# Three reorderings in a fused transformer kernel: shift after the first matmuls, attention steps of a mixer and of two layers

## The reference

```python
def first_block(...):                     # one layer
    mod = silu(c) @ w_ada + b_ada         # 9 vectors of 1024
    sh1, sc1, gt1, sh2, sc2, gt2, sh3, sc3, gt3 = split(mod)
    u = rmsnorm(h, g_norm_ffn1) * (1 + sc1) + sh1
    h = h + 0.5 * gt1 * swiglu(u, w_ffn1_in, w_ffn1_out)     # F = 2816
    u = rmsnorm(h, g_norm_mix) * (1 + sc2) + sh2
    h = h + gt2 * token_mixing(u, ...)    # pooling, and attention in 3 groups x 4 heads
    u = rmsnorm(h, g_norm_ffn2) * (1 + sc3) + sh3
    h = h + 0.5 * gt3 * swiglu(u, w_ffn2_in, w_ffn2_out)
    return rmsnorm(h, g_final)

def second_block(...):                    # two layers
    ret_o = retention(...)                # 4 heads, group norm: (o - mean) / sqrt(var + eps)
    swa_o = sliding window attention with sinks   # 6 query heads
    mla_o = latent attention, rope on 32 of 96 columns   # 6 heads
    x = layer_norm(ALPHA * x + concat(ret_o, swa_o, mla_o) @ w_out)
    x = layer_norm(ALPHA * x + grouped_moe(x))    # 16 experts, top 2
```

## Time and profile before

| | |
|---|---|
| median of 3 runs | 1138.8 us |
| lowest, highest | 1138.6, 1139.92 us |
| the profiled execution | 1139.93 us |
| its span in the trace | 1138.1 us |
| mean granted PE clock | 0.987 |
| PE busy | 1082.3 us |
| DVE busy | 876.1 us |
| ACT busy | 632.7 us |
| POOL busy | 90.1 us |

### The profile page before, as it was taken

How to read it: one execution, slowest core, us unless ns; L and a number is a source line. 1 busy time by engine, 2 the same in 40 slices (tenths; PEclk the granted TensorE clock), 3 DMA queues, 4 the chain that set the end, 5 groups by cost and what they waited for, 6 DMA issues and landing times.

```text
span 1138.1 us, 24969 instructions
## 1 busy us (share of the span) xinstructions
PE 1082.3 (95%) x10736; PEld 820.4 (72%) x10736; DVE 876.1 (77%) x1130; ACT 632.7 (56%) x792; POOL 90.1 (8%) x104
## 2 busy tenths in 40 slices
PE   6999999999889999999999998999989998999996
PEld 5777776688668477777678674877758876497773
DVE  4799799788667885555668856999966875699994
ACT  1554344454446564344466545878745754687872
POOL 1115611061000110000000000000000000000000
PEclk9999999999989999999999999999999999999998
DMA  9999799565436678655545225599994422569991
GB/s 340 372 368 374 268 344 360 177 218 187 161 135 223 201 254 285 219 193 161 152 166 203 77 75 226 181 384 414 414 281 128 158 100 86 222 223 398 416 374 39
DMA packets 134718, 271.94 MB, mean 239 GB/s; under 512 B 9429, under 2 KB 98105, under 8 KB 126297
## 3 DMA queue, kind: packets, MB, share of 16 engines
q1 hardware_dynamic: 124248, 231.79, 57.1%
q0 software_dynamic: 7904, 29.25, 7.3%
q10 hardware_dynamic: 2464, 9.44, 2.2%
HBM read 269.41 MB, written 1.05 MB: 238 GB/s over the span
## 4 chain that ended last, share of the span: by engine, by line
PE 77%; DVE 13%; ACT 4%; DMA 3%; issue 3%; ACTq 0%; DVEq 0%; SPq 0%
PE ps L750 64%; DVE wlo L469 4%; PE ps L1625 3%; DMA area<-in_w_ada_dram 2%; PE ps L1673 1%; PE ps L892 1%; PE ps L902 1%; DVE area L2842 1%; PE ps L910 1%; PE ps L1278 1%; DVE bnst L2283 1%; PE ps L1087 1%; PE ps L1290 1%; ACT area L1776 1%; PE ps L1125 0%
## 5 line engine op out<-in xcount | busy, mean ns | idle before, releaser
L469 DVE SCALAR_TENSOR_TENSOR wlo<-raw,whi 128x2048 f16<-128x2048 f32 (+4 forms) x212 | 466.4, 2231 | 31.6 <-ACT whi L444 31.0
L444 ACT ACTIVATE whi<-raw 128x2048 f16<-128x2048 f32 (+4 forms) x212 | 385.3, 1849 | 26.4 <-DMA raw<-in_w_ffn_in_dram 10.2
L750 PE MATMUL ps<-uhi,whi 128*128 128x256 f16 (+2 forms) x1328 | 329.8, 260 | 3.1 <-DVE ulo L2309 2.0
L750 PE MATMUL ps<-ulo,whi 128*128 128x256 f16 (+2 forms) x1328 | 329.6, 260 | 0.0
L750 PE MATMUL ps<-uhi,wlo 128*128 128x256 f16 (+2 forms) x1328 | 329.5, 260 | 0.0
L750 PE MATMUL ps<-whi,hreg 128*128 128x512 f16 (+1 forms) x656 | 206.6, 384 | 0.0
L750 PE MATMUL ps<-area,whi 128*128 128x96 f16 (+2 forms) x2168 | 155.1, 210 | 2.7 <-ACT area L1969 2.7
L750 PEld LDWEIGHTS ps<-area,whi 128*128 128x128 f16 (+2 forms) x2168 | 145.2, 99 | 15.5 <-issue 6.9
L750 PE MATMUL ps<-area,wlo 128*128 128x96 f16 (+2 forms) x1084 | 149.4, 210 | 0.0
L750 PEld LDWEIGHTS ps<-uhi,whi 128*128 128x128 f16 (+1 forms) x1328 | 130.4, 98 | 25.6 <-issue 9.0
L750 PEld LDWEIGHTS ps<-ulo,whi 128*128 128x128 f16 (+1 forms) x1328 | 130.2, 98 | 15.4 <-issue 1.9
(11 more groups left out here) (358 smaller groups left out, 1326.1 us busy)
## 6 DMA issues: line engine op xcount, KB each, us to landing
raw<-in_exp_w_gate_up_dram SPq DMA_DIRECT2D x64, 1024.0 KB, 8.4
raw<-in_w_ffn_in_dram SPq DMA_DIRECT2D x44, 1024.0 KB, 7.3
raw<-in_w_in_dram SPq DMA_DIRECT2D x34, 1024.0 KB, 6.7
area<-in_w_ada_dram POOLq DMA_DIRECT2D x48, 512.0 KB, 7.3
raw<-in_w_ffn_out_dram SPq DMA_DIRECT2D x22, 1024.0 KB, 7.8
raw<-in_exp_w_down_dram SPq DMA_DIRECT2D x22, 1024.0 KB, 9.6
raw<-in_w_out_dram SPq DMA_DIRECT2D x12, 1024.0 KB, 5.0
x<-in_exp_w_down_dram SPq DMA_DIRECT2D x6, 1024.0 KB, 10.6
```

The source lines that it names most:

```text
L444: act.activation(whi[:, u.slot, 0:n], raw[:, u.slot, 0:n], ACT.Copy, scale=SW)\
L469: dve.scalar_tensor_tensor(out=wlo[:, u.slot, 0:n], in0=raw[:, u.slot, 0:n], scalar=SW, in1=whi[:, u.slot, 0:n], op0=ALU.mult, op1=ALU.sub ...
L750: last = pe.matmul(o, st, mv, start=start and i == 0, stop=stop and i == 2, skip_group_check=True)
```

## The change

It has three parts.

1. **Prologue and chunk 0 of the first FFN.** The ACT queue loads the scale (now b = 0) in two parts, x, and the scale's other two parts. The shift (b = 1) goes to the SP queue behind units 0 and 1. DVE splits both units ahead of the scale columns; `norm_out(0)` uses the scale with a zero shift, into `u0hi` and `u0lo`, and chunk 0's stage1 runs on these. Between its two sides PE does `ada_direct(1)`, behind them `shift_sums`. When the shift is known, PE multiplies it with the same weights (`shift_biases`, 96 matmuls of one column), which gives chunk 0's missing term as a bias that `first_chunk` adds on ACT and DVE. `norm_out(1)` makes the shifted tokens for chunks 1 to 10. The warming matmuls between the steps of the prologue go down to four and six.
2. **Mixer 1.** `mix_scores(1, 2)`, the last scores of the second pair of heads, run ahead of `mix_values(0)`. On ACT weight splits 12 and 13 go behind `mix_turned(0)` and `(1)`, and the exponentials of heads 2 and 3 ahead of units 15 and 16. On DVE maxima of heads 2 and 3 come earlier and unit 15 (sums of w_ada) goes behind `mix_normal(2)` and `(3)`.
3. **Each of the two layers.** `rot_mla(0)`, `rope_mla(0)` and `ukv_keys(0)` go ahead. The group norm of retention goes ahead of the last normalisation, of `turned(5)` and of unit `OUT`; `pair_lo(5)` goes behind it.

The diff, cut to its core:

```diff
-ADA_STARTED = 13
+ADA_STARTED = 14
...
+        u0hi, u0lo = (gt[:, i, :].bitcast(F16).rearrange("p (k n) -> p k n", k=KT) for i in range(2))
...
-        def ada_first(eng, b):
-
-            for j in (0, 3, 1, 2):
-                eng.dma_start(first_w[b][j], w_ada[:, 2 * j:2 * j + 2, b * D:(b + 1) * D]).then_inc(ada_in[b][j], 16)
+        def ada_first(eng, b, js):
+
+            c0 = (M_SC1, M_SH1)[b]
+            for j in js:
+                eng.dma_start(first_w[b][j], w_ada[:, 2 * j:2 * j + 2, c0:c0 + D]).then_inc(ada_in[b][j], 16)
...
-                    sp.wait_ge(ada_sum, 6)
+                    ada_first(sp, 1, (0, 3, 1, 2))
+                    sp.wait_ge(ada_sum, 7)
...
-            def stage1(u, ph_banks, norm=None):
+            def stage1(u, ph_banks, norm=None, x16=None, side1=None):
+                xh, xl = x16 or (uhi, ulo)
                 for side in range(2):
                     pe.wait_ge(lo_made, (u + side).count(1))
+                    if side and side1 is not None:
+                        side1()
                     s_ = (u + side).slot
                     for ft in range(2):
                         for k in range(KT):
@@ -767,7 +778,20 @@
                                 norm_tiles(norm, k)
                             w = slice(k * 256 + ft * P, k * 256 + ft * P + P)
                             last = split_mm(ps[:, ph_banks + side, ft * T:(ft + 1) * T], whi[:, s_, w], wlo[:, s_, w],
-                                            uhi[:, k, :], ulo[:, k, :], k == 0, k == KT - 1)
+                                            xh[:, k, :], xl[:, k, :], k == 0, k == KT - 1)
+                    if x16 is None:
...
+            def shift_biases(u):
+
+                for side in range(2):
+                    s_ = (u + side).slot
+                    for ft in range(2):
+                        for k in range(KT):
+                            w = slice(k * 256 + ft * P, k * 256 + ft * P + P)
+                            c = 2 * side + ft
+                            last = split_mm(ps[:, 7, c:c + 1], whi[:, s_, w], wlo[:, s_, w], sh16[:, 0, k:k + 1],
+                                            sh16[:, 1, k:k + 1], k == 0, k == KT - 1)
...
-                    open_y()
-                    for _ in range(5):
-                        pe.matmul(ps[:, 3, :], ident16, zeros16[:, :], start=False, stop=False, skip_group_check=True)
-                    stage1(Unit(ph.u0), 4, 0)
+                    stage1(Unit(ph.u0), 4, 0, (u0hi, u0lo), lambda: ada_direct(1))
+                    shift_sums()
+                    pe.wait_ge(sh1_made, 2)
+                    shift_biases(Unit(ph.u0))
...
+                    if q is None and isinstance(c, int) and c == 1:
+                        stage1(u, 6, 1, None, lambda: pe.wait_ge(bias_out, 1))
+                        pe.wait_ge(h_made, 2)
+                        open_y()
...
+            def shift_sums():
+                pe.wait_ge(ada_sum, 13)
+                ada_ones(1, range(4))
+                pe.wait_ge(ada_sum, 14)
+                ada_ones(1, range(4, 8)).then_inc(mod_mm, 1)
...
-            ada_ones(0, range(8))
-            pe.wait_ge(diag_made, 2)
-            stay_warm(12, 1)
-            transposes(0)
-            ada_direct(1, 2)
-            stay_warm(5, 1)
-            pe.wait_ge(ada_sum, 12)
-            ada_ones(1, range(4))
-            pe.wait_ge(ada_sum, 13)
-            ada_ones(1, range(4, 8)).then_inc(mod_mm, 1)
-            stay_warm(5, 1)
+            ada_ones(0, range(4))
+            pe.wait_ge(ada_sum, 7)
+            ada_ones(0, range(4, 8)).then_inc(mod_mm, 1)
+            stay_warm(6, 4)
...
             mix_scores(1, 1)
+            mix_scores(1, 2)
             mix_values(0)
             gate_part(2, 1)
-            mix_scores(1, 2)
...
+                rot_mla(0)
                 uq(1)
                 values(1)
                 uq(2)
+                weights(UKV)
+                ukv_keys(0)
                 turn(2)
                 ret_scores(0)
-                rot_mla(0)
-                weights(UKV)
-                ukv_keys(0)
                 ukv_keys(1)
                 values(2)
...
+            def first_chunk(u_b):
+                act.wait_ge(used, u_b.count(1))
+                act.activation(bias0[:, :], ps[:, 7, 0:4], ACT.Copy, scale=1.0 / S).then_inc(bias_out, 1)
+                act.wait_ge(bias_out, 1)
+                act.wait_ge(u_lo, 8)
+                for ft in range(2):
+                    c = slice(ft * T, (ft + 1) * T)
+                    last = act.activation(s_act[:, c], ps[:, 4, c], ACT.Silu, scale=1.0 / S, bias=bias0[:, ft:ft + 1])
+                last.then_inc(silu_made, 1)
...
-            ada_first(act, 0)
+            ada_first(act, 0, (0, 3))
             for t in range(TT):
                 act.dma_start(x[:, t, :], a["x"][0, t * P:(t + 1) * P, :]).then_inc(x_in, 16)
+            ada_first(act, 0, (1, 2))
             act.wait_ge(vec_t, 1)
             act.activation(cond[:, :], ps[:, 3, 0:8], ACT.Silu).then_inc(cond_made, 1)
-            ada_first(act, 1)
             act.wait_ge(used, RING)
             act.wait_ge(stack_in, 16 * 20)
             rms_first()
             hi_part(act, Unit(0))
+            hi_part(act, Unit(1))
             act.wait_ge(mod_cols, 1)
-            norm_out(0, acol[:, 0, :], adacols[:, 0:8])
-            for i in range(1, AHEAD):
+            norm_out(0, acol[:, 0, :], zero8[:, :])
+            for i in range(2, AHEAD):
                 hi_part(act, Unit(i))
+            act.wait_ge(sh1_made, 1)
+            norm_out(1, acol[:, 0, :], adacols[:, 0:8])
...
-            unit1(12)
-            unit1(13)
             mix_turned(0)
             gate_out(1)
             mix_turned(1)
-            unit1(14)
+            for i in (12, 13, 14):
+                unit1(i)
             mix_out_hi(0)
+            mix_exps(2)
+            mix_exps(3)
             gate_out(2)
             unit1(15)
             unit1(16)
...
-                turned(5)
-                unit(OUT)
                 act.wait_ge(ret_oc, l + 1)
                 act.activation(osq, ocen, ACT.Square).then_inc(ret_std, 1)
-                pair_hi(5)
                 act.wait_ge(ret_var, l + 1)
                 act.activation(stat[:, 48:56], stat[:, 40:48], ACT.Sqrt, scale=1.0 / 64,
                                bias=small[:, C_EPSLN:C_EPSLN + 1]).then_inc(ret_std, 1)
+                turned(5)
+                unit(OUT)
+                pair_hi(5)
...
+            def first_chunk():
+                dve.wait_ge(silu_made, 1)
+                for ft in range(2):
+                    c = slice(ft * T, (ft + 1) * T)
+                    ins = dve.tensor_scalar(h_f32[:, c], ps[:, 5, c], 1.0 / S, bias0[:, 2 + ft:3 + ft], ALU.mult, ALU.add)
+                link(ins)
+                dve.scalar_tensor_tensor(out=h_f32, in0=h_f32, scalar=SX, in1=s_act, op0=ALU.mult, op1=ALU.mult).then_inc(h_made, 1)
...
-            ada_first_sums(0, (0, D))
+            ada_first_sums(0, range(4))
+            rms_xn(0)
+            ada_first_sums(0, range(4, 6))
...
-            ada_first_sums(1, (0, HALF, D), range(2))
-            rms_xn(0)
-            ada_first_sums(1, (0, HALF, D), range(2, 6))
             lo_part(dve, Unit(0))
+            lo_part(dve, Unit(1))
...
-            shift_columns(0, ps[:, 2, 0:8], B_SH1)
-            scale_columns(0, ps[:, 2, 8:16], B_SC1, V_G1)
-            norm_split(0)
-            for i in range(1, AHEAD):
-                lo_part(dve, Unit(i))
+            scale_columns(0, ps[:, 6, 0:8], B_SC1, V_G1)
+            norm_split(0, u0hi, u0lo)
+            ada_first_sums(1)
+            lo_part(dve, Unit(2))
+            dve.wait_ge(mod_mm, 2)
+            shift_columns(0, ps[:, 6, 8:16], B_SH1)
+            dve.wait_ge(dve_step, n_step[0])
+            dve.tensor_copy(sh16[:, 0, :], adacols[:, 0:8]).then_inc(sh1_made, 1)
+            dve.wait_ge(sh1_made, 1)
+            dve.tensor_tensor(sh16[:, 1, :], adacols[:, 0:8], sh16[:, 0, :], ALU.subtract).then_inc(sh1_made, 1)
+            norm_split(1, uhi, ulo)
...
             unit1(12)
+            mix_masked(1, (0,))
             unit1(13)
-            mix_masked(1, (0, 1))
-            unit1(14)
-            mix_out_lo(0)
-            mix_masked(1, (2,))
+            mix_masked(1, (1, 2))
             mix_maxima(2)
             mix_maxima(3)
-            unit1(15)
+            mix_out_lo(0)
+            unit1(14)
             mix_normal(2)
             mix_normal(3)
+            unit1(15)
...
+                rope_mla(0)
+                normal(2)
                 unit(UQ)
-                normal(2)
                 pair_lo(1)
                 turned(2)
                 decayed(0)
                 decayed(1)
-                rope_mla(0)
...
-                normal(5)
-                pair_lo(4)
-                turned(5)
                 dve.wait_ge(ret_o, 4 * l + 4)
```

(35 more changed lines are left out.)

66 lines of the change are left out of this document (33 added, 33 removed).

## The result

The changed kernel takes 1132.79 us (median, 1132.19 to 1133.73), beside 1138.98 for the kernel before (1138.6 to 1140.86). The ratio is 0.9943, 95% interval 0.9928 to 0.9957: faster by 6.2 us. The profiled execution took 1133.07 us with a span of 1131.3, 6.8 us less than the span before. The forecast was 1130.1, so the sign was right and the gain was some 70% of what was said.

The account below looks back on a forecast made before the run. PE was taken as the bound, busy 1082.3 of 1138.1 us, with DVE close behind. 1139.93 + 11.6 - 7.5 - 12.8 = 1131.2, 1130.1 as a median; range 1123 to 1137 by its bounds, 1115 to 1141 leaving out 2 in 10.

Parts of the forecast that it names:

- M: Prologue: time at which the scale columns are ready on DVE, taken as 30.7 us against 39.6 before, 8.9 earlier.
- DVE's lateness: First FFN: DVE reaches the lo part of unit 5 9.9 us late, 2.4 of clock cost included.
- That it isn't given back: First FFN: DVE's 7.29 us stall moves along with DVE, so its 9.9 us delay stands in full on the gt row.
- rival A: First FFN: DVE's delay is absorbed and only PE's own of about 4 us is left; 1122.5 us, chance 0.25.
- PE's own lateness: First FFN: PE itself some 4 us late by the gt row, 2.3 of new work and an estimated 1.7.
- estimated 1.7 at the down of chunk 5: First FFN: PE delay of 1.7 us at chunk 5's down, whose lo part DVE makes behind 132.82.
- The wait at the gt row and its clock: First FFN: PE delayed 9.8 us at the gt row, waiting some 5 us there; lowered clock behind it costs 1.8.
- +11.6: Prologue and first FFN together: net loss of 11.6 us, from +7.5 to +15.5.
- Mixer 1 and the layers: Reordered attention: waits of PE and half clock behind them go, -7.5 us in mixer 1 and -6.4 in each layer.
- rival C: Attention: reorderings only move the stalls, half of the 20.3 us gain remains; 1140.2 us, chance 0.12.
- Rival B: Prologue: PE stays at the lower clock from chunk 0's first matmul until the biases are through; 1144.5 us, chance 0.13.
- for more than 15 of them: Sign of being wrong: PE in the first 60 us shows clock 0.5 for more than 15 us.

Follow-up runs that it names:

- tables: The changed kernel with POOL's rope tables in four pieces behind ada blocks 3 to 6 instead of one piece behind block 3: 1125.45 us.
- attn: The kernel before with parts 2 and 3 of the change (mixer 1 and both layers) and without part 1: 1116.48 us, ratio 0.9794.
- pad: The kernel of attn with 120 matmuls of 16 columns on zeros added where PE is idle, and four warming matmuls less: 1116.32 us.
- attn_tables: The kernel of attn with POOL's rope tables in four pieces instead of one: 1117.18 us, ratio 0.9799 to the kernel before.
- fill: The changed kernel with twenty more warming matmuls in PE's idle gap ahead of chunk 0: 1128.46 us, ratio 0.9886 to the kernel before.
- rope: The kernel before with only rot_mla(0), rope_mla(0) and ukv_keys(0) moved ahead in both layers, group norm left as it was: 1137.13 us, ratio 0.9972.

## Why the prediction was right, and where it was off

**The prologue's columns.** M = 30.7 was said, 30.58 came. The arithmetic of bytes over 368 GB/s and the splits in a row on ACT and DVE held.

**DVE's lateness.** 9.9 us was said, 10.2 came (68.03 less 57.87). The parts: side 0 ended at M + 10.2 (8.9 + 1.4 said), ada_direct took 3.47 (3.5), side 1 6.93 (5.3 + 1.0), the sums 1.70 (1.8). Behind the sums DVE took 15.1 us to the lo part of unit 5 (15.15 said).

**That it isn't given back.** The step that mattered most, and the one against rival A: DVE's stall follows POOL, POOL follows DVE. It came as said (7.13 us, 10 us later), and the tables run took the link away and got 7 to 8 us back. That is near what rival A would have been (1125.45 measured, 1122.5 said); it needed another kernel.

**PE's own lateness.** "Some 4 us" was too little. In the changed kernel the first matmul of `down` starts at 70.39 (64.30 before), 6.1 us late, and PE is just as late when it stops for the gt row (206.68 - 3.94 = 202.74, against 196.65); the tables run, with DVE out of the way, has 5.6 at the FFN's end. The two terms of the "4" were both off. The estimated 1.7 at the down of chunk 5 did not come, as PE has no wait between 54 and 202. The piece that the sum left out is the third fall, during chunk 1's stage1 (0.50 in 56 to 60), behind the column sums and the 96 one-column matmuls of the biases: the 96 matmuls of that stage1 took 13.4 us instead of 10.6. It did not change the result, as DVE was the bound.

**The wait at the gt row and its clock.** PE's delay to that point was put at 9.8 and is 10.0. But the half clock behind it was sized at 1.8 us and cost 4.4: 2.6 in the 96 matmuls, 0.9 in the 32 passes and 0.95 in the two behind them (13.24, 4.36 and 1.92 against 10.64, 3.47 and 0.97). This is the term that makes most of the miss: +14.5 instead of +11.6. The price was taken from 24 matmuls in the mixer alone, without the transposes ahead of them, with which the prediction itself puts the same slow stretch at 2.3. And it left out the fall at the FFN's end, which in the changed kernel covers the passes and the two behind them.

**Mixer 1 and the layers.** -8.2 for -7.5 and -7.3 for -6.4 per layer. The mechanism was right in each place and rival C fell: no wait that replaced an old one is longer than 0.4 us. In the layers the term that was left out is PE's second wait of 0.51, ahead of the turning, which the move of `normal(2)` nearer to its inputs took away too.

**The gap between the layers** was in no step: +1.5 us.

**How much of the nearness was luck.** The misses are +2.9 in the first FFN and +1.5 between the layers, and -0.7, -0.9 and -1.0 in the mixer and the layers. They cancel to +1.8, so the total is nearer than its parts. The bounds don't add up as they were written either: all upper ones together give 1138.8 + 15.5 - 3 - 8 = 1143.3 and not 1137, and the lower one of the first FFN, without a clock term and with M at 30.2, is 6.9 without the 1.8 behind the gt row and 8.7 with it, not 7.5. The result lies inside in any case.

**Rival B** would have needed the lower clock from the first matmul of chunk 0 until the biases. It was there from 31 to 38 (PE idle until 33), around 45 to 48 and from 55 on to 62, and came back to full each time in between. Of the first 60 us these are 15.3, so the sign "for more than 15 of them" was met by a hair, although the price up to the sums was near the one said (2.9 us in the two sides for 2.4): the sign was set too low for what it was to tell. The Trainium skill ("TensorE: Matmul & The Clock Gate", HAM oscillation) lays such falls to gaps in PE's work; the trace agrees for the gaps of 5.58 us and of 3.94 us at the gt row, and goes beyond it for the falls at 45 and 55, where PE had no gap, or only 0.7 us, and at 222, where it had none.

The change as a whole is a gain of 23 us and a loss of 17 or 18 put together. The version that leaves the prologue as it was, attn, is the fastest that was tried, 1116.5 us (pad and attn_tables, built on it, are level with it). That part 1 started the first real matmul 9 us earlier did nothing for it, as the work behind it grew by more on the engine that has 0.1 us of slack later. From the columns to the lo part of unit 5 DVE took 18.2 us before and takes 37.4 now: it makes the shift's sums there, waits 6.98 us for PE's column sums, and splits the tokens a second time.

## What to carry to other kernels

An earlier start of the bound engine is worth only what the next engine's total allows. Before you add work to that engine, look for the place with the least slack further down the same phase, and for idle time that looks like a reserve but hangs on the same engine's progress. In these runs the half clock behind a stall of PE went when the stall went (mixer 1, the group norm), and the new stall at the gt row brought one. Price a new one from the work that will stand behind that very gap, not from another. And measure the parts of a compound change by themselves, since a sum of -6 can be -23 and +17.

## What was not expected of the hardware

The granted clock fell to 0.50 without an idle gap, during or right behind stretches of one-column matmuls of 3.5 to 4.3 us, and did so in some profiles and not in others (1.00 in attn, 0.68 in attn_tables behind the same 32 passes). The unchanged prologue varies too: 0.50 in 40 to 44 in attn, 1.00 in before. The three kernels with more warming matmuls spread by 8 to 10 us from run to run (fill 1125.03 to 1134.6), the changed kernel by 1.5; but rope, with the prologue of before, spread by 7.4, and before itself by up to 6.0 in a group.

DVE was slower beside POOL's table work: four ada sums took 4.09 us beside it and 3.11 without it, three unit splits 7.41 instead of 6.69, in before as in after. Where the tables were in pieces (tables, attn_tables) the slower rows moved with the pieces.
